# Sixteen to 64 bytes between the high and the low half of each block of `ya`, in six output stages

## What is computed

```
h = h + mix @ w_out
u = rms_norm(h, mlp_norm_g)
h = h + square(relu(u @ w_up)) @ w_down          # w_up 2048 x 8192, w_down 8192 x 2048
...
x = x + (y * silu(gate)) @ mla_w_out             # 2048 x 2048
x = x + (y * silu(gate)) @ swa_w_out             # 2048 x 2048
```

## The kernel before, in words

| tensor | stages that stream it | row | gap |
|---|---|---|---|
| `ya` | one tile in four of merge; the down stages, mla_out, swa_out | 2144 | 0 |
| `ux` | the up stages, the input projections of both attention blocks | 2144 | 0 |
| `yb` and `mx` | one tile in four of merge; the stage out | 2048 | 0 |
| `u` (its last 256 tokens) | two tiles in four of merge, among others | 2176 | 64 |

## Time and profile before

### The profile page before, as it was taken

One profiled execution on the slowest core, in us unless ns is written; L12 is line 12 of the kernel. 1 busy time (PEld: TensorE's weight loads), 2 busy tenths in 40 slices (PEclk: granted clock), 3 DMA queues, 4 the chain that ended last, 5 costly groups with the idle time before them and its releaser, 6 DMA issues.

```text
span 2748.1 us, 50879 instructions
## 1 busy us (share of the span) xinstructions
PE 2717.4 (99%) x17597; PEld 2457.1 (89%) x17597; DVE 2032.3 (74%) x3698; ACT 1417.0 (52%) x2469; POOL 310.3 (11%) x323
## 2 busy tenths in 40 slices
PE   7999999999999999999999999999999999999998
PEld 7999999999998888888888888888888998888887
DVE  7888888888888566567765666656777767788875
ACT  6566566656655434334443544534545455455553
POOL 0000000000000000004700000000460002400024
PEclk9999999999999999999999999999999999999999
DMA  6444444444444555556566555655555544544445
GB/s 226 147 155 146 156 149 151 156 139 160 148 151 144 177 189 187 189 189 215 177 194 192 184 193 181 194 190 182 195 183 177 164 166 159 188 164 142 146 154 183
DMA packets 130236, 472.74 MB, mean 172 GB/s; under 512 B 15136, under 2 KB 15136, under 8 KB 129952
## 3 DMA queue, kind: packets, MB, share of 16 engines
q1 hardware_dynamic: 126144, 457.37, 51.1%
q0 software_dynamic: 3936, 13.34, 1.6%
HBM read 468.40 MB, written 2.25 MB: 171 GB/s over the span
## 4 chain that ended last, share of the span: by engine, by line
PE 96%; DVE 2%; ACT 1%; issue 1%; DMA 0%; DVEq 0%; SPq 0%; ACTq 0%
PE bank L318 41%; PE bank L319 21%; PE bank L320 8%; PE bank L322 8%; PE bank L321 7%; PE bank L902 1%; PE bank L857 1%; PE bank L911 1%; DVE w_lo L294 1%; PE bank L1126 1%; PE bank L1286 1%; PE bank L969 0%; PE bank L1203 0%; ACT w_hi L288 0%; PE bank L1302 0%
## 5 line engine op out<-in xcount | busy, mean ns | idle before, releaser
L294 DVE TENSOR_TENSOR w_lo<-raw,w_hi 128x1024 fp32r<-128x1024 f32 x862 | 1058.7, 1253 | 159.1 <-ACT w_hi L288 156.5
L288 ACT ACTIVATE w_hi<-raw 128x1024 fp32r<-128x1024 f32 x862 | 896.2, 1052 | 430.1 <-PE bank L319 424.0
L318 PE MATMUL bank<-ya,w_hi 128*128 128x512 f32 x1792 | 625.3, 393 | 0.7 <-DVE h L2273 0.7
L318 PE MATMUL bank<-ux,w_hi 128*128 128x512 f32 x1744 | 621.1, 398 | 0.1
L319 PE MATMUL bank<-ya,w_lo 128*128 128x256 f32 x1792 | 500.9, 279 | 0.0
L319 PE MATMUL bank<-ux,w_lo 128*128 128x256 f32 x1744 | 487.6, 280 | 0.0
L320 PE MATMUL bank<-u,w_hi 128*128 128x272 f32 (+1 forms) x1296 | 408.3, 315 | 4.8 <-DVE u L445 2.9
L318 PEld LDWEIGHTS bank<-ya,w_hi 128*128 128x128 f32 x1792 | 336.6, 188 | 77.3 <-issue 2.2
L318 PEld LDWEIGHTS bank<-ux,w_hi 128*128 128x128 f32 x1744 | 327.6, 188 | 74.1 <-issue 2.9
L322 PE MATMUL bank<-u,w_lo 128*128 128x272 f32 (+1 forms) x1296 | 373.2, 288 | 0.0
L321 PE MATMUL bank<-u,w_hi 128*128 128x272 f32 (+1 forms) x1296 | 372.8, 288 | 0.0
(11 more groups left out here) (422 smaller groups left out, 3831.0 us busy)
## 6 DMA issues: line engine op xcount, KB each, us to landing
raw<-in_stream SPq DMA_DIRECT2D x864, 512.0 KB, 3.4
mix_row<-rows POOLq DMA_DIRECT2D x16, 408.0 KB, 4.9
xT<-in_xT SPq DMA_DIRECT2D x4, 544.0 KB, 5.6
mix_coef_m<-meta_rows POOLq DMA_DIRECT2D x16, 128.0 KB, 3.4
h<-in_xT POOLq DMA_DIRECT2D x1, 2048.0 KB, 9.7
out_dram<-h SPq DMA_DIRECT2D x8, 256.0 KB, 2.4
consts<-in_consts POOLq DMA_DIRECT2D x1, 1817.0 KB, 11.7
meta_rows<-mix_b_mat POOLq DMA_DIRECT2D x16, 1.0 KB, 3.6
```

Of the source, the lines that this page charges most:

```text
L288: act.activation(w_hi[:, slot], raw[:, slot], ACT.Copy).then_inc(hi_ready, 1)
L294: dve.tensor_tensor(w_lo[:, slot], raw[:, slot], w_hi[:, slot].bitcast(F32), ALU.subtract).then_inc(lo_ready, 1)
L318: pe.matmul(o, a, x, start=first, stop=False)
```

## The change

In six stages (down0 to down3, mla_out, swa_out) the operand x lies in the same region of SBUF as before, but its rows and gaps differ from stage to stage. `ROWS` holds one view for each:

| stage | row, bytes | gap, bytes | start |
|---|---|---|---|
| down0 | 2144 | 32 | `ya_at` |
| down1 | 2144 | 48 | `ya_at` |
| down2 | 2144 | 16 | `ya_at` |
| down3 | 2112 | 32 | `ya_at` |
| mla_out | 2080 | 16 | `ya_at` |
| swa_out | 2176 | 64 | `ya_at` - 512 |

Writers (ScalarE for the high half, VectorE for the low half) and reader (TensorE) of a stage use the same view. The merge stage still streams `ya` without a gap, and the up stages stream `ux` as before. No instruction is added, removed or moved: on each of the five engines the lists of instructions of both kernels agree in number, order and shape, and only addresses and names differ. Where the two halves touched, the 512 columns were one run of addresses; with a gap they are two runs of 256, as they were for `u` all along.

```diff
+        def rows_of(name, where, row, gap):
+
+            both = place(name, [P, KT, row], F32R, where)[:, :, 0:2 * (SEQ + gap)]
+            return both.rearrange("p k (a n) -> p k a n", a=2)[:, :, :, 0:SEQ]
+
+        ROWS = {"down0": rows_of("rows_down0", ya_at, BLOCK, 8),
+                "down1": rows_of("rows_down1", ya_at, BLOCK, 12),
+                "down2": rows_of("rows_down2", ya_at, BLOCK, 4),
+                "down3": rows_of("rows_down3", ya_at, 2 * SEQ + 16, 8),
+                "mla_out": rows_of("rows_mla", ya_at, 2 * SEQ + 8, 4),
+                "swa_out": rows_of("rows_swa", ya_at - 512, 2 * SEQ + 32, 16)}
...
-                matrix(f"down{q}", ya, ("hidden lo", (q + 1) * KT, 1))
+                matrix(f"down{q}", rows_for(f"down{q}"), ("hidden lo", (q + 1) * KT, 1))
...
-                act.activation(ya_x[:, k, 0, :], sum_t[:, s, None, :], ACT.Copy).then_inc(sem("hidden hi"), 1)
+                act.activation(ROWS[f"down{q}"][:, k, 0, :], sum_t[:, s, None, :], ACT.Copy).then_inc(sem("hidden hi"), 1)
...
-                dve.tensor_tensor(ya_x[:, t, 1, :], sum_t[:, s, None, :], ya_x[:, t, 0, :].bitcast(F32),
+                o = ROWS[f"down{q}"]
+                dve.tensor_tensor(o[:, t, 1, :], sum_t[:, s, None, :], o[:, t, 0, :].bitcast(F32),
                                   ALU.subtract).then_inc(sem("hidden lo"), 1)
...
-            matrix("swa_out", ya, ("swa lo", KT, 1), begun=True)
+            matrix("swa_out", rows_for("swa_out"), ("swa lo", KT, 1), begun=True)
```

More of the change, by code:

```diff
@@ L360, in ya, with rows_for, x @@
             return ya_x[:, k]
+        def rows_for(stage):
+            def x(k):
+                return ROWS[stage][:, k]
+            return x
         def yb(k):
@@ L1226, in _ @@
             for w in range(windows(MLA_UNIT, PAIRS, MLA_PE)):
-                stream_ = mla_products(w) if w < PAIRS else first_blocks("mla_out", ya, ("mla lo", PAIRS - 1))
+                stream_ = mla_products(w) if w < PAIRS else first_blocks("mla_out", rows_for("mla_out"), ("mla lo", PAIRS - 1))
                 steps = window(MLA_PE, w, MLA_UNIT, PAIRS) if w < PAIRS else [(at, w, step) for at, *step in MLA_PE_END]
@@ L1236, in _ @@
                     pass
-            matrix("mla_out", ya, ("mla lo", HEADS // 2, 2), begun=True)
+            matrix("mla_out", rows_for("mla_out"), ("mla lo", HEADS // 2, 2), begun=True)
             for t in range(SWA_KV_TILES):
@@ L1308, in _ @@
                         "out": swa_out}
-            out_left = first_blocks("swa_out", ya, ("swa lo", BEGUN_BLOCKS))
+            out_left = first_blocks("swa_out", rows_for("swa_out"), ("swa lo", BEGUN_BLOCKS))
             for w in range(windows(SWA_UNIT, KT, SWA_PE)):
@@ L1744, in mla_y_hi @@
                 act.wait_ge(sem("mla y"), n)
-                act.activation(ya_x[:, 2 * n - 2:2 * n, 0, :], y_v[:], ACT.Copy).then_inc(sem("mla hi"), 1)
+                act.activation(ROWS["mla_out"][:, 2 * n - 2:2 * n, 0, :], y_v[:], ACT.Copy).then_inc(sem("mla hi"), 1)
             steps_act = {"evac": mla_evac, "evac qr": mla_evac_qr, "tanh": mla_tanh,
@@ L1796, in swa_y_hi @@
                 act.wait_ge(sem("swa y"), n)
-                act.activation(ya_x[:, bass.ts(n - 1, 1), 0, :], s_y[:, None, :], ACT.Copy).then_inc(
+                act.activation(ROWS["swa_out"][:, bass.ts(n - 1, 1), 0, :], s_y[:, None, :], ACT.Copy).then_inc(
                     sem("swa hi"), 1)
@@ L2428, in mla_y_lo @@
                 t = slice(2 * n - 2, 2 * n)
-                dve.tensor_tensor(ya_x[:, t, 1, :], y_v[:], ya_x[:, t, 0, :].bitcast(F32),
+                o = ROWS["mla_out"]
+                dve.tensor_tensor(o[:, t, 1, :], y_v[:], o[:, t, 0, :].bitcast(F32),
                                   ALU.subtract).then_inc(sem("mla lo"), 1)
@@ L2507, in swa_y_lo @@
                 t = bass.ts(n - 1, 1)
-                dve.tensor_tensor(ya_x[:, t, 1, :], s_y[:, None, :], ya_x[:, t, 0, :].bitcast(F32),
+                o = ROWS["swa_out"]
+                dve.tensor_tensor(o[:, t, 1, :], s_y[:, None, :], o[:, t, 0, :].bitcast(F32),
                                   ALU.subtract).then_inc(sem("swa lo"), 1)
```

## The result

The changed kernel takes 2755.94 us (median of 15), the kernel before 2750.73 us on the same chips; the ratio is 1.0017 with a 95% interval of 1.0010 to 1.0023. It is 0.17% slower, inside the range, on the side of rival B, and short of the 0.2% that was called the measurement's limit. One execution of each kernel took far longer (5441.36 us before, 11286.89 us after) and is left out of what follows, so that fourteen remain of each.

A forecast was written before the change was run, and what follows sets the result against it. TensorE's distance between matmul starts was taken as the bound (busy 99% of 2748.1 us). Terms of 0.3 us (down3) and 0.64 us (swa_out), all others 0, gave +0.9 us on 2750.35: 2751.3 us, range 2744.5 to 2756.0 us.

The forecast's parts named there:

- rival B: Six stages: a gap makes TensorE start its stream anew at column 257; 2.5 ns a product, 2754.2 us; chance 0.18.
- The writers' term of 0: ScalarE and VectorE writing the halves of x: only the destination's start moves, so their writes cost 0.
- the start of each block: Six stages, where x's blocks begin against loading weights: +0.3 us in down3, +0.64 us in swa_out, 0 elsewhere.
- the two offsets of `u`: swa_out: row 2176 was said to give its blocks the offsets of `u`, hence +2.5 ns a product, +0.64 us.
- the 4 ns between `mx` and `u`: Paces of 354 and 350.0 ns; if the difference is the gap's alone, the six stages win 6.1 us.
- the gap: I take 0: Long matmul of six stages: a load of 128 columns lies mostly under the first half, so the gap costs 0.
- The bounds: Six stages: a product takes between 342 and 354 ns, which is -8.4 to +10.0 us for the gap.
- Rival A: Six stages: the gap helps, taking away meetings with the weight stream in the second half; -4.5 us, 2745.9 us; chance 0.2.
- Rival C: Six stages: pace hangs on where the tensor lies, not its rows; all keep 347.5 ns, 2750.35 us; chance 0.12.

## Why the prediction was right, and where it was not

**The bound was read rightly.** TensorE's waits, and ScalarE's and VectorE's load, are unchanged, and the whole cost lies in the distance from start to start. The writers' term of 0 held: 418 and 426 ns before, 418 and 426 after.

**Step "the start of each block".** The reading, a meeting of the stream of x with the loading weights, is shown by the moved weights (mx 353.1 to 346.7 ns) and by all moved together (no pace changed). The terms drawn from it were partly right. swa_out was forecast at 350.0 ns from the rows of `u` and had 350.0, but partly by luck: the prediction gives it "the two offsets of `u`", and it has not got them. The tensor `u` begins at a multiple of 256 bytes from the others, but its last 256 tokens, which are what is streamed, begin 16 tokens, 64 bytes, later. So the high halves of `u` lie 64 and 192 bytes on, modulo 256, and those of swa_out 0 and 128. Row and gap are the same, the place is not; at row 2048 a start of 0 and one of 64 happen to have the same pace too. The two that were reasoned, not read, were wrong in size: mla_out's row "steps through the same eight offsets in another order, 0" costs 3.3 ns without any gap, and down3's row 1.7 rather than 1. Rows 2080 and 2144 step through the same eight places and differ by 3.3 ns, so the set of places does not make the pace. The 354 ns of `mx` was ten products of a rhythm that repeats every three; the whole rhythm has 353.3, so the bound was a little wide and the 4 ns between `mx` and `u` were 3.

**Step "the gap: I take 0".** This step failed. Gaps of 32, 48 and 16 bytes cost 1.7, 1.3 and 5.0 ns on row 2144, 0.47 + 0.32 + 1.24 = 2.0 us of the 4.3. With 0.8, 0.9 and 1.7 ns in down3, mla_out and swa_out, the gaps make some 2.8 us, and the rows the rest. The argument for 0, that a load lies mostly under the first 256 columns, was named an inference and is refuted by the table of gaps: moving only the second half of x changes the pace by -1.6 to +5.0 ns. The bounds held for what was forecast: every stage of the changed kernel lies between 342 and 354 ns, and so do all 30 or so layouts tried in the six stages. They are not bounds for every layout: `u` with the high weights moved has 356 ns.

**Rival B** had the right sign and nearly the time (2754.2 us; like for like the changed kernel is at 2750.35 + 4.3 = 2754.65), but its mechanism, a fixed price for a second run of addresses, is refuted: on row 2176 a gap of 32 bytes is a gain of 1.6 ns. Its 2.5 ns a product averaged with other numbers to about the same. **Rival A**, that a gap helps, is right for that one layout, 2176 with 32, and for none that the change picked. **Rival C**, that the place and not the rows make the pace, is half right: the place does, and rows are one way to set it.

The forecast of +0.9 us was thus a fifth of the true +4.3, and the bounds from the nearest rows, not the forecast, kept the time inside the range.

**Open.** The rule by which distance becomes pace was not found: no smooth function of the start fits 353.1, 346.7, 353.4, 350.0, 351.2, 346.7, 353.3, 353.3. What decides between the two patterns of a layout, and whether another spacing of the weight blocks would do better than 344.4 ns, was not tried. That the two reads of TensorE meet in SBUF is the reading left after the runs; they show that the distance of the addresses sets the pace, not what happens inside the memory.

## What to carry to other kernels

Where TensorE is the bound, measure its pace from start to start and set it against the columns over the clock; here 320 ns of columns cost 344 to 356, by layout alone. Treat the place of the moving operand against the weight buffers, modulo 256 bytes, as something to be tuned by trial, several layouts per run, one in each stage that repeats exactly; price a layout only by a row of that same layout, for neither a single product nor an argument about overlaps carried over; and even such a row can be 6.4 ns off, where a layout has two patterns. "The same layout" means the address of the slice that is streamed, not that of its tensor. And when two profiles differ by a little, look first for where the difference begins: 1.6 of 6.0 us began here before the first changed line.

## What the runs showed of the hardware

- The pace of matmuls whose weights change each time depends on the distance between the addresses of the moving operand and of the weights: 344.4 to 353.3 ns for 512 + 256 columns in the stages at a granted clock of 1.00, and 356 ns for `u` in merge with the high weights moved. A period of 256 bytes in the start was seen three times (0 and 256, 32 and 288, 64 and 320).
- The pace of a given layout repeats in other stages, with other matrices (352.5 and 349.2 ns, twice each), and moving all operands together leaves it (eight of eight).
- Two layouts ran at two paces each, 346.7 and 353.1 ns, 344.4 and 346.7 ns.
- With every block in the same place modulo 256 (`mx`, row 2048), the starts repeat every three products, not every one: 1.06 us for three. The same layout in down0 needs 1.06 us whether VectorE and ScalarE work or not.
- A gap of 16 to 64 bytes within the moving operand is neither free nor of a fixed price: -1.6 to +5.0 ns for each 512 columns. By the Trainium skill ("SBUF — State Buffer", Door 1: The DMA port swizzle) an access pays when it crosses to a new line of 16 bytes. A gap of whole lines adds no such crossing, so by that rule alone all these gaps would be free; the trace does not agree.
- One wait of 1.9 us in the same place was followed by the lower clock (0.65 of full speed, averaged over 3.5 us, against 1.00) in some executions and not in others, at a cost of 1.6 us.
